# First mixer in another order, and the opening scale vector on TensorE

## The reference

```python
mods = (silu(c) @ w_ada + b_ada).reshape(B, 9, D)          # shift, scale, gate x 3
n = rmsnorm(h, g_pre[0]) * (1 + scale(0)) + shift(0)
h = h + 0.5 * gate(0) * rmsnorm(swiglu(n, ...), g_post[0])  # stage F0

n = rmsnorm(h, g_pre[1]) * (1 + scale(1)) + shift(1)        # stage M1, the first mixer
qa, ka, va, qi, ki, wi, qb, kb, vb = split(n @ w_in)
ki = rmsnorm(ki, g_kidx)
# a: score = sum_h relu(qi_h . ki) * wi_h ; top 64 keys of a query; bias by distance; softmax; times va
# b: z = qb . kb / 8 ; u = log_sigmoid(-z) under a strict causal mask ; between = reversed cumsum(u) - u ;
#    A = exp(log_sigmoid(z) + between) ; times vb
o = concat(rmsnorm(oa, g_out_a), rmsnorm(ob, g_out_b)) @ w_out
h = h + gate(1) * rmsnorm(o, g_post[1])
...                                                         # F1, then the second block F2, M2, F3
```

## Time and profile before

| | |
|---|---|
| median of 3 runs | 1205.73 us (1204.8 to 1206.36) |
| profiled execution, own time | 1206.5 us |
| its span, first to last instruction | 1204.4 us |
| mean granted TensorE clock | 0.972 |
| TensorE busy | 1111.2 us, 92% of the span |
| VectorE busy | 823.0 us, 68% |
| ScalarE busy | 503.7 us, 42% |
| transfers | 266.94 MB, 222 GB/s over the span |

### The profile page before, as it was taken

One profiled execution on the slowest core, in us unless ns is written; L12 is line 12 of the kernel. 1 busy time (PEld: TensorE's weight loads), 2 busy tenths in 40 slices (PEclk: granted clock), 3 DMA queues, 4 the chain that ended last, 5 costly groups with the idle time before them and its releaser, 6 DMA issues.

```text
span 1204.4 us, 17844 instructions
## 1 busy us (share of the span) xinstructions
PE 1111.2 (92%) x7042; PEld 1003.0 (83%) x7042; DVE 823.0 (68%) x859; ACT 503.7 (42%) x552; POOL 40.5 (3%) x76
## 2 busy tenths in 40 slices
PE   4399999979998989999999999997999988999997
PEld 2299999869897779999978999996788767999996
DVE  6578988664786477777667787768655567655554
ACT  2244334436635353443444433433445344343342
POOL 0000000010110000000020000001000000000000
PEclk9999999979997899999989999999999999999999
DMA  8879998625322559888648999724443263766651
GB/s 325 326 261 390 371 362 286 196 70 168 125 86 71 175 178 345 313 304 289 210 167 308 359 335 330 264 104 169 159 140 113 97 212 120 245 223 219 204 191 53
DMA packets 144966, 266.94 MB, mean 222 GB/s; under 512 B 9641, under 2 KB 103958, under 8 KB 139670
## 3 DMA queue, kind: packets, MB, share of 16 engines
q1 hardware_dynamic: 143024, 262.96, 62.8%
q0 software_dynamic: 1056, 3.17, 0.8%
q10 hardware_dynamic: 838, 0.15, 0.1%
HBM read 263.60 MB, written 2.65 MB: 221 GB/s over the span
## 4 chain that ended last, share of the span: by engine, by line
PE 79%; DVE 9%; DMA 4%; ACT 4%; issue 1%; SPq 1%; POOL 1%; POOLq 0%; DVEq 0%; ACTq 0%
PE ps L1617 14%; PE ps L1620 14%; PE ps L1619 14%; PE ps L1573 11%; PE ps L1574 10%; PE ps L1575 10%; DVE w_lo L1003 2%; DVE nT L1015 1%; DMA arena<-in_w_ada 1%; ACT w_hi L678 1%; DMA toe_scratch<-arena 1%; DMA arena<-in_ffn_w_up 1%; ACT y_row L691 1%; ACT arena L862 1%; DVE y_row L1140 1%
## 5 line engine op out<-in xcount | busy, mean ns | idle before, releaser
L1003 DVE TENSOR_TENSOR w_lo<-w_raw,w_hi 128x2048 fp32r<-128x2048 f32 (+2 forms) x170 | 382.5, 2253 | 219.5 <-ACT w_hi L678 219.2
L678 ACT ACTIVATE w_hi<-w_raw 128x2048 fp32r<-128x2048 f32 (+2 forms) x170 | 319.8, 1885 | 337.9 <-PE ps L1575 159.4
L1617 PE MATMUL ps<-nT_hi,w_hi 128*128 128x256 f32 x1424 | 404.2, 284 | 0.0
L1619 PE MATMUL ps<-nT_lo,w_hi 128*128 128x256 f32 x1424 | 403.6, 283 | 0.0
L1620 PE MATMUL ps<-nT_hi,w_lo 128*128 128x256 f32 x1424 | 403.5, 283 | 0.0
L1617 PEld LDWEIGHTS ps<-nT_hi,w_hi 128*128 128x128 f32 x1424 | 273.9, 192 | 1.8
L1619 PEld LDWEIGHTS ps<-nT_lo,w_hi 128*128 128x128 f32 x1424 | 273.9, 192 | 1.6
L1620 PEld LDWEIGHTS ps<-nT_hi,w_lo 128*128 128x128 f32 x1424 | 273.9, 192 | 0.0
L1573 PE MATMUL ps<-w_hi,hT_hi 128*128 128x512 f32 x328 | 128.5, 392 | 0.0
L1082 DVE SCALAR_TENSOR_TENSOR arena<-arena,c_act 128x3072 f32<-128x3072 f32 (+2 forms) x49 | 128.1, 2649 | 0.0
L1574 PE MATMUL ps<-w_lo,hT_hi 128*128 128x512 f32 x328 | 128.1, 390 | 0.0
(11 more groups left out here) (237 smaller groups left out, 978.7 us busy)
## 6 DMA issues: line engine op xcount, KB each, us to landing
arena<-in_w_ada SPq DMA_DIRECT2D x16, 1536.0 KB, 7.9
arena<-in_ada_w SPq DMA_DIRECT2D x16, 1536.0 KB, 7.1
w_raw<-in_w_in SPq DMA_DIRECT2D x46, 512.0 KB, 4.7
w_raw<-in_w_ffn_down SPq DMA_DIRECT2D x44, 512.0 KB, 4.7
w_raw<-in_ffn_w_down SPq DMA_DIRECT2D x44, 512.0 KB, 4.3
w_raw<-in_w_ffn_gate SPq DMA_DIRECT2D x42, 512.0 KB, 6.3
w_raw<-in_w_ffn_up SPq DMA_DIRECT2D x42, 512.0 KB, 7.5
w_raw<-in_ffn_w_gate SPq DMA_DIRECT2D x42, 512.0 KB, 4.2
```

The costliest lines, as they stand in the source:

```text
L678: copy = lambda o, i: act.activation(o, i, ACT.Copy)
L1003: dve.tensor_tensor(lo(s, n), raw(s, n), hi(s, n).bitcast(F32), ALU.subtract).then_inc(lo_ready[s], 1)
L1617: pe.matmul(o, hi(s)[:, cols], nT_hi[:, kk, :], start=(half == first_half and k == 0 and i % 2 == 0), stop=False, skip_group_check=True)
L1619: pe.matmul(o, hi(s)[:, cols], nT_lo[:, kk, :], start=False, stop=False, skip_group_check=True)
```

## The change

The opening: the eight transfers alternate between shift and scale (`FIRST`). VectorE sums only the shift. The scale vector comes out of TensorE, by 64 float32 matmuls whose weights are 128 columns of the loaded `w_ada` rows and whose moving operand is one column of `c_act`; a buffer that held scale rows is free when `scale_mm` says so. F0's third weight piece is issued ahead of the store of the bias table, and SyncE waits no longer for that store. ScalarE's and VectorE's splits are interleaved with the norm's copies.

The mixer: `GROUPS1` is now vb, qi, qb, kb, ka, qa, va. The first group, values of part b, is taken tile by tile, tile 0's rows between the two tiles' transposes. The index keys and scores follow at once, then qb, kb, one half of ka, z, the other half, qa, r, the logits, one half of va, times vb, the other half, and the softmax. Halves after the index keys are taken 1, 0. `bias` is added into `u_sb` before the logits, u goes to `e_sb`, and the logits stay in `u_sb`. Of the b half of the output product a quarter moves behind the a half's transposes. The splits on ScalarE and VectorE move accordingly.

```diff
-            "start": [(0, 0, 0, 0), (D, 0, 1, 0)],
+            "start": [(0, 0, 0, 0)],
+        FIRST = [(0, 0), (0, 1), (1, 0), (0, 2), (1, 1), (0, 3), (1, 2), (1, 3)]
-        GROUPS1 = [("qb", 2120), ("kb", 2632), ("qi", 1536), ("ka", 512), ("vb", 3144), ("qa", 0), ("va", 1024)]
-        KI = 3
+        GROUPS1 = [("vb", 3144), ("qi", 1536), ("qb", 2120), ("kb", 2632), ("ka", 512), ("qa", 0), ("va", 1024)]
+        KI = 1
...
+            def load_first(i):
+                if i >= 3:
+                    m, q = FIRST[i - 3]
+                    sp.wait_ge(scale_mm if m else first_sum, q + 1)
...
             load_gu("F0", 0, 0)
             load_gu("F0", 1, 0)
+            load_gu("F0", 0, 1)
...
-            sp.wait_ge(toe_stored, 16)
-            for half in range(2):
-                sp.wait_ge(ada_done[half], 4)
             ffn_loads("F0", lambda: group1(0, 0), lambda: group1(0, 1))
...
             split_hi(*gate_up("F0", 0, 0))
+            norm_hi("F0", 0, range(1))
             split_hi(*gate_up("F0", 1, 0))
+            norm_hi("F0", 0, range(1, PAIRS))
             split_hi(*gate_up("F0", 0, 1))
-            for t in range(T):
-                norm_hi("F0", t, range(PAIRS))
+            norm_hi("F0", 1, range(PAIRS))
```

ScalarE's queue in the mixer, after:

```diff
+            transposed_group(3, TKB)
+            for h in range(H):
+                act.wait_ge(z_mm, h + 1)
+                act.activation(z_sb[:, h, :], ps[:, 4 + h % 4, 0:CAUSAL], ACT.Copy, scale=DH ** -0.5).then_inc(z_out, 1)
+            split_hi(*piece1(0, 4))
+            act.wait_ge(z_out, H)
+            act.activation(e_sb[:], z_sb[:], ACT.Abs).then_inc(z_ln, 1)
+            act.wait_ge(z_ln, 1)
+            act.activation(e_sb[:], e_sb[:], ACT.Exp, scale=-1.0).then_inc(z_ln, 1)
+            split_hi(*piece1(1, 5))
+            act.wait_ge(z_ln, 2)
+            act.activation(e_sb[:], e_sb[:], ACT.Ln, bias=1.0).then_inc(z_ln, 1)
+            transposed_group(4, TKA)
+            split_hi(*piece1(0, 5))
+            split_hi(*piece1(1, 6))
+            transposed_group(5, TQA)
+            split_hi(*piece1(0, 6))
             act.wait_ge(loga_ready, 1)
             act.activation(z_sb[:], z_sb[:], ACT.Exp).then_inc(a_exp, 1)
```

VectorE's, from the top-k on:

```diff
+            split_lo(*piece1(0, 2))
+            dve.wait_ge(score_causal, 1)
+            topk(0, 3)
+            split_lo(*piece1(1, 3))
+            topk(3, 6)
+            split_lo(*piece1(0, 3))
+            topk(6, TOPK // 8)
...
+            split_lo(*piece1(1, 4))
...
+            split_lo(*piece1(0, 4))
+            split_lo(*piece1(1, 5))
+            dve.wait_ge(z_ln, 3)
+            dve.scalar_tensor_tensor(e_sb[:], z_sb[:], 0.0, e_sb[:], ALU.max, ALU.add).then_inc(u_ready, 1)
+            split_lo(*piece1(0, 5))
+            split_lo(*piece1(1, 6))
             for h in range(H):
                 dve.wait_ge(r_mm, h + 1)
                 dve.tensor_tensor(z_sb[:, h, :], z_sb[:, h, :], ps[:, 4 + h % 4, 0:CAUSAL], ALU.subtract).then_inc(r_out, 1)
             dve.wait_ge(r_out, H)
             dve.tensor_scalar(z_sb[:], z_sb[:], 0.0, None, ALU.min).then_inc(loga_ready, 1)
             split_lo(*piece1(0, 6))
+            for h in range(H):
+                dve.wait_ge(l_mm, h + 1)
...
```

And TensorE's:

```diff
             pe.wait_ge(vec_ready, 2)
+            def scale_piece(q):
+                i = FIRST.index((1, q))
+                pe.wait_ge(first_loaded[i % 3], 16 * (i // 3 + 1))
+                for row in range(2):
+                    for k in range(KD):
+                        at = row * D + k * P
+                        last = pe.matmul(ps[:, 0, k:k + 1], first_raw[:, i % 3, at:at + P], c_act[:, 0, 2 * q + row:2 * q + row + 1],
+                                         start=(q == 0 and row == 0 and k == 0), stop=(q == 3 and row == 1), skip_group_check=True)
+                last.then_inc(scale_mm, 1)
+            pe.wait_ge(c_ready, 1)
+            for q in range(3):
+                scale_piece(q)
             norm_transposes("F0", 0)
             pe.wait_ge(pick_ready, 1)
             sum_folds("start")
+            scale_piece(3)
             ffn("F0")
...
+            for t in range(T):
+                norm_transposes("M1", t)
+                order = (0, 1) if t == 0 else (1, 0)
+                for n, half in enumerate(order):
...
+            group_half(4, 1)
+            pe.wait_ge(grp_out, 8)
...
+                pe.matmul(ps[:, 4 + h % 4, 0:S], k[:, 0:P], q, start=True, stop=True, skip_group_check=True)
...
+            group_half(4, 0)
+            group_free(5)
+            group_half(5, 1)
+            group_half(5, 0)
...
+            row_group(s1, banks[1], NB, None, 4, start=True, ks=(0, 1))
             pe.wait_ge(o_ready, 1)
             pe.wait_ge(pT_out, H)
             out_transposes(0, 6)
+            row_group(s1, banks[1], NB, None, 4, ks=(2, 3)).then_inc(w_used[s1], 1)
```

More of the change, by code:

```diff
@@ L1216, in _ @@
                         norm_row("F0", t)
-            for half in range(2):
-                dve.wait_ge(ada_done[half], 4)
-            fold(first_acc, D, folds[:, 1, :]).then_inc(folded, 1)
+            dve.wait_ge(first_sum, 4)
+            fold(first_acc, 0, folds[:, 0, :]).then_inc(folded, 1)
+            mods_out("start")
             split_lo(*gate_up("F0", 0, 0))
-            split_lo(*gate_up("F0", 1, 0))
-            mods_out("start")
-            for t in range(T):
-                norm_cols("F0", t, 0)
-                for pair in range(1, PAIRS):
-                    norm_cols("F0", t, pair)
-                    norm_lo("F0", t, pair - 1)
-                norm_lo("F0", t, PAIRS - 1)
+            dve.wait_ge(scale_mm, 4)
+            link(dve.tensor_tensor(mod_col[:, 0, 0, :], ps[:, 0, 0:KD], vec_col[:, 0, KD:2 * KD], ALU.add))
+            link(dve.scalar_tensor_tensor(mod_col[:, 0, 0, :], mod_col[:, 0, 0, :], 1.0, vec_col[:, 0, 72:72 + KD], ALU.add, ALU.mult))
+            norm_cols("F0", 0, 0)
+            norm_cols("F0", 0, 1)
+            norm_lo("F0", 0, 0)
+            norm_lo("F0", 0, 1)
+            split_lo(*gate_up("F0", 1, 0))
+            for pair in (2, 3):
+                norm_cols("F0", 0, pair)
+                norm_lo("F0", 0, pair)
+            norm_cols("F0", 1, 0)
+            for pair in range(1, PAIRS):
+                norm_cols("F0", 1, pair)
+                norm_lo("F0", 1, pair - 1)
+            norm_lo("F0", 1, PAIRS - 1)
             ffn("F0", piece1(0, 0))
@@ L1364, in _ @@
             dve.sem_inc(o_ready, 1)
+            split_lo(*out1[0, 0])
             out_half(6, 0, 2, nT)
@@ L1807, in _ @@
                           skip_group_check=True).then_inc(idx_mm, 1)
-            value_half(4, 0)
+            group_free(2)
+            group_half(2, 1)
+            group_half(2, 0)
+            group_free(3)
+            group_half(3, 1)
+            group_half(3, 0)
+            group_free(4)
+            group_half(4, 1)
+            pe.wait_ge(grp_out, 8)
+            for h in range(H):
+                if h >= 4:
+                    pe.wait_ge(z_out, h - 3)
+                else:
+                    pe.wait_ge(idx_relu, h + 5)
+                q, k = head(TQB, h), head(TKB, h)
+                pe.matmul(ps[:, 4 + h % 4, 0:S], k[:, 0:P], q, start=True, stop=True, skip_group_check=True)
+                pe.matmul(ps[:, 4 + h % 4, S:CAUSAL], k[:, P:S], q[:, P:S], start=True, stop=True,
+                          skip_group_check=True).then_inc(z_mm, 1)
+            group_half(4, 0)
+            group_free(5)
+            group_half(5, 1)
+            group_half(5, 0)
             pe.wait_ge(u_masked, 2)
```

280 lines of the change are left out of this document (116 added, 164 removed).

## The result

The changed kernel takes 1210.24 us (median of 12 runs, 1205.43 to 1215.16) where the kernel before, run beside it on the same chips, takes 1205.13 (12 runs). The ratio is 1.0038, 95% interval 1.002 to 1.0055: 5.1 us slower by the medians. The profiled execution happens to be the slowest of the 12. Timed once more beside later experiments, it has a ratio of 1.0066: the loss is 5 to 8 us. In the whole record two executions, of 1583.25 and 2200.7 us, lie far outside their kernels' usual times, and the ratios leave them out.

What follows compares the result with a forecast made beforehand. The prediction took F0 as bound by TensorE end to end, so a later start is paid in full. Opening +6.4 and M1 +2.0 gave +8.4, so 1214.1 us, range 1203 to 1221.

Steps and rivals of the forecast that it cites:

- my sum: Whole kernel: the prediction's own added terms, +8.4 us to 1214.1, own range 1209 to 1219, chance 60 in 100.
- The opening: +6.4 forecast: Ahead of F0: scale pieces of 6.8 us each move the start of F0's rows from 50.32 to 56.7.
- the wait of the sixth: Opening: the sixth weight transfer waits for scale piece 0 to free its buffer; the queue idles seven microseconds.
- the first rival: Opening: a scale piece costs only 3.6 us, rows start at 47.0, time 1204.4, not slower; 15 in 100.
- Values by tile: M1's entry: tile 0's value rows fill TensorE's 6.8 us hole, so both halves end 6.4 us earlier.
- The middle: M1, from the values to the first transposes of probabilities: new waits lengthen it by 13.7 us.
- z's wait: M1's middle: TensorE waits 4.8 us after the z products for splits queued behind ScalarE's z copies.
- the fifth head's: M1's logits: four heads run ahead, then the fifth waits 3.5 us for VectorE.
- the score's ones: M1's index scores: waits behind copies, score sums and top-k, among them 1.2 and 1.3 us.
- The index keys' 1.4: M1's middle: VectorE's folds and small split come after tile 1's norm, costing a wait of 1.4 us.
- the three waits of 1.15: M1's logits: each of the three heads after the fifth waits 1.15 us.
- Probabilities and output rows: M1's end: probabilities gain 2.5 us (bounds 0 and 6), output rows moved into a wait gain 2.8.

Runs made afterwards that it cites:

- the opening alone: Every edit of the opening with the old first mixer, against the kernel before: 1212.39 us, ratio 1.0063.
- the second comparison: The changed kernel unaltered, timed and profiled once more against the kernel before: 1211.54 us, ratio 1.0066; its profile is the second profile.
- The run with the other order: The changed kernel with tile 1's value rows taken half 0 first, then half 1: 1209.56 us, ratio 1.0045 to the kernel before.
- the mixer alone: The old opening with the new first mixer, against the kernel before: 1203.90 us, ratio 1.0006.
- the early weight piece without it: The kernel before with F0's third weight piece fetched ahead of the bias table's store, splits interleaved, VectorE still summing shift and scale: 1197.77 us, ratio 0.9949.

## Why the prediction held, point by point

**Direction and cause: right.** Slower was forecast with a chance of 0.73, by the opening above all, and the experiments put the loss there: 8.1 us for the opening alone, nothing measurable for the mixer. The forecast of +8.4 stands against +8.3 in the profiled execution and 8.1 between the medians of the second comparison, but against 5.1 between those of the first; 1214.1 is 3.9 above the median 1210.24, which lies inside the range and inside my sum's own 1209 to 1219. The close match of the spans is in good part luck, as the terms show.

**The opening: +6.4 forecast, 5.0 at the first rows, 5.9 from tile 1's rows on.** The price, 6.8 us a piece, was right (6.84 from 37.24 to 44.08), and so were the gate (22.83, forecast 23.2), the hole in the transfers and the wait of the sixth. What was off is small: the seventh transfer landed at 37.2, not 38.2, and the transposes with the fold product took 2.1 us, not 2.6. The Trainium skill, "TensorE: Matmul & The Clock Gate", section LDWEIGHTS, gives a weight load as its columns over 1.2, 107 ns for 128, which as an estimate, with two loads a matmul, makes a piece 3.4 us. The trace does not agree: it has 6.84, and half the matmuls had to be left out to reach 3.4. By the Trainium skill, the same page, Part 1, sustained activity releases the throttle. The trace does not agree for the scale pieces: three of them, 22.8 to 44.2 us with one gap of 0.6, kept one price. No run has a matmul of one column at the high level, so the other price stays unmeasured. One sum of mine has a slip: 16 matmuls of 0.21 are 3.4 us, not the 3.6 of the first rival, whose rows would start some 0.6 earlier; nothing else hangs on it.

**Values by tile: -6.4 forecast, -2.4 measured.** I set the start of tile 1's rows by the entry to F1, where half 0 comes first and waits 1.23 for one column pair. Here half 1 comes first, needs the last two pairs and waits 3.17. The run with the other order shows that term, 2.0 us. The rest is rows at the low clock, and that is chance: in the second profile they ran at 1.00, and the index keys' first product came 2.9 us earlier.

**The middle: +13.7 forecast, 15.0 in the windows, by two errors that cancel.** z's wait was forecast at 4.8 and is 4.80; the fifth head's at 3.5 and is 3.56; the score's ones at 1.2 and 1.3 and are 1.27 and 1.11. The index keys' 1.4 did not come, because the late values covered it, and `split_hi(1,5)` cost 1.2 instead of 2.9, since the half before it ran in part at the low clock (7.4 us, where the next one took 6.0) and used up the rest; the three waits of 1.15 between the later heads did not come either, since the logits there ran at the low clock (1.22 us a pair of records instead of 0.70) and filled them. So TensorE's idle time grew by 8.5 us (5.7 to 14.2), where my sum has 13.2 (8.7 to 21.9). Its busy time grew by 6.5, where my sum has 0.5. The low clock is what I priced too low: by its mean, 0.08 of 125.5 against 0.05 of 110.5 is 4.5 us more, where I had 2.2 behind the logits against 2.4 before, and nothing behind z. The causal masks cost nothing in the change, as forecast, but their cover is thin: they end 1.85 us ahead of the first r product, and once the splits are out of the way they are the last link of the chain behind z.

**Probabilities and output rows: -5.3 forecast, -12.1 measured.** This is the largest miss. I expected some heads at the high clock and took 2.5; all eight ran at 1.00 and gave 7.1 (15.8 to 8.7), beyond my bound of 6. The output product gave 5.1 rather than 2.8, since it had started at 0.50 before. The mechanism that I named (ScalarE's copies come at once) is real, with 0.25 us of wait in place of two holes. But it is not shown to be what raised the clock: with a hole put back by experiment the clock stayed at 1.00. Most of the 12.1 us is thus clock whose cause stays open.

**Together.** M1 was forecast at +2.0 and is +0.3 in this profile, -0.5 in the second and +2.3 in that of the mixer alone, whose times show nothing. Misses of +4.0, +1.3 and -6.8 nearly cancel, and that is luck. The rest of the 8.3, some 2 us, arises behind M1. The second profile of the same kernel, at clock 0.980, is 0.9 us ahead of the first at the end of M1 (428.87), 2.3 at tile 1's rows of F1 (440.42 after 442.74) and 3.5 at the end. My "give or take 1 us of clock" was too small. Over the first 12 runs the span is 1203.0 at clock 0.985 and 1212.7 at 0.976. A mean 0.009 lower is 11 us of full-rate work (0.009 x 1212), and 9.7 us is what the spans differ by.

## What to carry to other kernels

Price an operation that moves onto the critical engine at the pace that the engine has at that moment, and then follow what waits for its end: here a buffer freed 7 us late stopped the queue that all weights come through, and with the same work started 7 us earlier the rows began ahead of the kernel before (48.95 against 50.32), though still behind the early weight piece without it (42.38). When several waits in a row are all for one engine's queue, moving one instruction removes a wait and hands most of it to the next; compute the chain through to the next product before counting the gain. And separate the parts of a mixed change: one part of this one alone gives 7 us, and another takes it away.

## What the runs showed of the hardware

The column of granted clock reads 1.00 throughout the opening, but the pace is that of the low level, 1.2 GHz: a float32 matmul of one column with 128x128 weights of its own takes 0.43 us, 512-column float32r matmuls go at 0.43 us each there and at 0.23 later. Some 28 us of scale pieces between 22.8 and 53.1 changed nothing in this, and starting them at 16.0 didn't either (the rows at 48.95 still began at 0.43). The pace rose 6.3 us after the 512-column rows began (at 61.6), and 5.3 us after they began in the kernel before, where TensorE had been nearly idle ahead of them. So in the opening the pace must be read from the distance between records.

In M1 a hole of 1.8 us with busy stretches ahead left the clock at 1.00, and holes of 4.8 and 6.3 were followed by products at the low level. Behind the hole of 3.2 us ahead of tile 1's value rows the first profile has the low level and the second the high one. The clock of one and the same code is thus not fixed: in these two profiles the window from 260 to 270 has 0.66 and 1.00.
